# Layer norms of a six-block network on one core: the squares summed by token quarters, the root and its inverse on 128 columns, the inverse spread by a product, the gate columns summed last

## The chip, the cores and the metric

The kernel runs on one core of one Trainium2 chip. The metric is the device time of one launch in microseconds (us), the median of three runs. The matrix engine is called PE here (its weight loads PEld), the vector engine DVE, the scalar engine ACT, GpSimd POOL, and the queue of weight loads SP. Memory in front of PE's output is PSUM, in banks of 128 partitions by 512 float32 values.

## The reference, cut to what matters

A residual stream x of 512 tokens by 1024 channels goes through four mixer layers (MLA, sliding window, sparse, MLA), a norm, and then two blocks of a second network (hybrid attention and state space with a context of 256 tokens, FFN, short convolution, FFN). In front of each of the eight sublayers x is normed over its channels and modulated:

```python
def rmsnorm(x, g):
    xf = x.astype(jnp.float32)
    y = xf * lax.rsqrt(jnp.mean(xf * xf, axis=-1, keepdims=True) + RMS_EPS)
    return (y * g.astype(jnp.float32)).astype(x.dtype)
...
        shift, scale, gate = jnp.split(cond @ ada_w[i] + ada_b[i], 3, axis=-1)
        h = rmsnorm(x, norm_g[i]) * (1 + scale[:, None, :]) + shift[:, None, :]
...
        x = x + gate[:, None, :] * y
```

There are two more norms of x without modulation (the end of the first network and of the second), one of the context, and in each MLA layer two small ones (of q_a with 256 channels and of kv_a with 128). All values are float32.

## The kernel before, in words

x lies with channels on partitions: eight tiles of 128 channels by 512 tokens. A mean over channels is therefore a sum over partitions, and PE makes it: a product of a 128 by 128 matrix of ones with the squares puts each token's sum on all 128 partitions of a PSUM bank, 512 columns wide. The trace records each float32 product as two MATMUL passes, so a line with x2 is one product.

Each engine has its program written out by hand, in order, and semaphores connect them. What happens at the border between two sublayers, where the change lies:

- The last product of a sublayer (`out_projection`, or the FFN's down chunks) makes x tile by tile. DVE adds each tile to x (`add_result`, L2206), ACT squares it (L1599), and DVE adds up the squares of tiles 0 to 6 in `sq_sum`.
- `result_squares` on PE (L767 to L782) sums `sq_sum` with the ones (L770), then four columns of the modulation, then the squares of the last tile (L778) into the same bank. The modulation columns (`column_sums`, L751) are the next sublayer's shift, scale and gate: POOL has summed weight times condition over the channel tiles in `ada_sum`, and PE sums each of 24 blocks of 128 over its partitions. Columns 0 to 15 are shift and scale, 16 to 23 the gate, which is not needed before the end of the sublayer. All 24 go into one tile. Two products of the identity (`fill`, L764) follow, whose result nothing reads.
- ACT takes the root of the 512 columns (`root_of_squares`, L1609), DVE the reciprocal (`normed`, L2052, or `final_norm`, L2067) into the bank RB. Then DVE adds the biases to the 24 columns (`mod_columns`, L2042), makes the gains (L2044), and makes h in eight steps of 128 by 512 (L2061): x times gain times RB. ACT adds the shift to each (`shift`, L1531), and PE's next product waits for the first of them and takes the eight, one after the other.

`final_norm` of the first network is special: x is normed in place (L2072), ACT squares it again (L1519), PE sums each of the eight squares by itself (`sum_squares`, L746), then turns the context (L1415), which DVE copies, and sums its squares (L1419). Then DVE norms both (`normed(5)`, `normed(4)`), and ACT shifts both. In the MLA layers the two small norms take ones products at L925 and L709, reciprocals at L2229 and products of two tiles of the gate (`gate(0, i)`) between them and their use.

PE's product tiles go to two PSUM banks in turn (`next_tile`, `evacuated`, `tile_used`). POOL starts the next sublayer's modulation when DVE tells `mods_ready`; SP starts a weight load when PE tells `slot_begun`.

Of the kernel before, what the change touches and what calls it, by code (L numbers as in the profile page):

```python
# [19 lines left out]
P = 128  # L20
T = 512
D = 1024
KT = D // P
TT = T // P
CTX = 256
# [211 lines left out]
def build(nc, A, out, tables, const):  # L237

    ctx = ExitStack()
    with ctx:  # L240
# [92 lines left out]
        def view(first, *shape):  # L333
# [4 lines left out]
            if len(shape) == 3:  # L338
# [13 lines left out]
                 "ada_step", "ada_product", "mods_ready", "dve_step", "act_step", "sq_ready", "sq_done", "square_given", "sum_step", "sum_done", "rms_ready",  # L352
# [320 lines left out]
        def _(pe):  # L673
# [69 lines left out]
            def sum_squares(i, first=False, part=T):  # L743

                pe.wait_ge(S["sq_ready"], n.take("sq_ready"))
                pe.matmul(SB[0][:, 0:part], ones, sq[:, i % 2, 0:part], start=first, stop=True,  # L746
                          skip_group_check=True).then_inc(S["sq_done"], 1)
# [158 lines left out]
            def mla(first=False):  # L906
# [16 lines left out]
                for i in range(2):  # L923
                    pe.wait_ge(S["lora_sq"], n.take("lora_sq"))
                    m = pe.matmul(tile.at, ones, sq[:, i, :], start=(i == 0), stop=(i == 1))  # L925
                m.then_inc(S["tile_done"], 1)
                pe.wait_ge(S["lora_sq"], n.take("lora_sq"))
                product(lambda k: ones, lambda k: probs[:, 0, 0:T], 1)
                for i in range(2):
                    gate(0, i)  # L930
# [423 lines left out]
            def ffn(job):  # L1354
# [7 lines left out]
                                lambda k, i=i: sum0 + 3 * i + k) for i in range(2)]  # L1362
                first_parts(chunks[0], slot_begins=False, fresh=h0)
# [45 lines left out]
            def block2_tensor():  # L1409
                for k in range(KT):  # L1410
# [5 lines left out]
                    m.then_inc(S["tile_done"], 1)  # L1416
                for k in range(KT):
                    pe.wait_ge(S["sq_ready"], n.take("sq_ready"))
                    pe.matmul(SB[1][:, 0:CTX], ones, sq[:, k % 2, 0:CTX], start=(k == 0), stop=(k == KT - 1)  # L1419
                              ).then_inc(S["sq_done"], 1)  # L1420
# [6 lines left out]
                ffn(None)  # L1427

# [24 lines left out]
            first_columns()  # L1453
            pe.wait_ge(S["consts_in"], 16)
# [1391 lines left out]
```

## Time and profile before

| | |
|---|---|
| three runs | 3045.56, 3048.13 and 3053.22 us, median 3048.13 |
| the profiled execution | span 3043.8 us from first to last instruction |
| PE busy | 2856.9 us, 94% of the span |
| DVE, POOL, ACT busy | 45%, 35%, 22% |
| mean granted PE clock | 0.963 of full speed |

The profiled execution's own time is not listed beside its span; the span lies 4.3 us under the median of the runs. PE is busy nearly throughout, but a pass counts as busy whether or not its result is needed.

### The profile page before, as it was taken

How to read it: one execution, taken by the hardware profiler on the slowest of the kernel's cores; microseconds unless marked ns; L12 is line 12 of the kernel's file. 1: busy time of each engine (PE TensorE's matmuls, PEld its weight loads, DVE VectorE, ACT ScalarE, POOL GpSimd, SP SyncE). 2: the span in 40 equal slices, each digit the busy share in tenths (PEclk: the TensorE clock that was granted, in tenths of full speed). 3: DMA queues.
4: the chain of work that ended last, by engine and by line, in shares of the span. 5: the costliest groups of instructions: out<-in, count | busy, mean ns of one | idle time of the engine just before them, and what ended most of it. 6: DMA issues, size and time to landing. Idle time of an engine off the chain costs nothing.

```text
span 3043.8 us, 32692 instructions
## 1 busy us (share of the span) xinstructions
PE 2856.9 (94%) x11819; PEld 1879.8 (62%) x11819; DVE 1362.8 (45%) x2676; ACT 673.7 (22%) x1588; POOL 1071.6 (35%) x574
## 2 busy tenths in 40 slices
PE   6899999999999999998889978999999999999997
PEld 5455544475555544554557546578888544688886
DVE  7333366314555723334645155445365322433454
ACT  2232134122333411323223122211100100211101
POOL 4783484088370008805830000287000583000000
PEclk7999999989999999999898988999999999999999
DMA  7342342244231024322310100244222343222221
GB/s 235 119 128 79 105 127 72 82 136 118 77 97 35 15 83 128 114 70 77 93 46 14 55 14 14 90 153 144 87 89 87 125 158 104 69 83 91 89 87 66
DMA packets 244976, 278.21 MB, mean 91 GB/s; under 512 B 39251, under 2 KB 217696, under 8 KB 244736
## 3 DMA queue, kind: packets, MB, share of 16 engines
q1 hardware_dynamic: 215872, 175.56, 18.8%
q0 software_dynamic: 28224, 100.86, 10.3%
q8 instruction: 71, 1.16, 0.2%
q10 hardware_dynamic: 768, 0.30, 0.0%
q14 instruction: 41, 0.34, 0.0%
HBM read 274.59 MB, written 2.10 MB: 91 GB/s over the span
## 4 chain that ended last, share of the span: by engine, by line
PE 85%; DVE 6%; DMA 3%; issue 2%; ACT 2%; SPq 1%; POOL 1%; DVEq 0%; ACTq 0%; POOLq 0%
PE psum L709 26%; PE psum L1315 24%; PE psum L866 11%; PE psum L852 3%; PE psum L736 3%; PE psum L840 3%; PE psum L1142 2%; PE psum L1190 2%; PE psum L751 1%; PE psum L1160 1%; PE psum L990 1%; PE psum L991 1%; DMA ring<-in_ffn_w_gate 1%; PE psum L1282 1%; PE psum L1195 1%
## 5 line engine op out<-in xcount | busy, mean ns | idle before, releaser
L709 PE MATMUL psum<-h,ring 128*128 128x512 f32 (+1 forms) x1808 | 772.3, 585 | 23.3 <-ACT h L1531 16.6
L636 POOL DMA_DIRECT2D ada_ring<-in_ada_w x192 | 114.7, 597 | 1446.7 <-DVE gains L2044 1223.5
L709 PEld LDWEIGHTS psum<-h,ring 128*128 128x128 f32 x1808 | 343.3, 193 | 417.4 <-issue 407.0
L648 POOL TENSOR_SCALAR ada_ring<-ada_ring,cond 128x1024 f32<-128x1024 f32 x168 | 481.9, 2869 | 8.6 <-POOL ada_sum L652 1.9
L652 POOL TENSOR_TENSOR ada_sum<-ada_sum,ada_ring 128x1024 f32<-128x1024 f32 x168 | 395.8, 2356 | 14.9
L866 PE MATMUL psum<-og,ring 128*128 128x512 f32 x768 | 334.6, 595 | 2.3 <-DVE og L2574 2.0
L1315 PE MATMUL psum<-og,arena 128*128 128x256 f32 x1152 | 258.6, 379 | 1.7 <-ACT probs L1882 1.7
L866 PEld LDWEIGHTS psum<-og,ring 128*128 128x128 f32 x768 | 145.1, 191 | 183.0 <-issue 179.5
L1315 PEld LDWEIGHTS psum<-og,arena 128*128 128x128 f32 x1152 | 218.7, 190 | 32.1 <-issue 2.4
L1315 PE MATMUL psum<-h,ring 128*128 128x256 f32 x768 | 178.3, 383 | 0.9 <-ACT h L1531 0.9
L1555 ACT ACTIVATE psum<-psum,neg_max 128x256 f32<-128x256 f32 (+4 forms) x288 | 150.1, 521 | 111.8 <-DVE neg_max L2126 85.4
L1566 ACT ACTIVATE probsT<-psum 128x128 f32<-128x128 f32 (+3 forms) x232 | 104.2, 449 | 300.3 <-PE psum L840 299.5
L1315 PEld LDWEIGHTS psum<-h,ring 128*128 128x128 f32 x768 | 145.6, 191 | 26.9 <-ACT h L1531 4.9
L1599 ACT ACTIVATE sq<-x 128x512 f32<-128x512 f32 x63 | 39.7, 630 | 428.9 <-DVE x L2206 232.7
L1882 ACT ACTIVATE probs<-psum 128x256 f32<-128x256 f32 x132 | 50.5, 383 | 369.7 <-PE psum L1315 369.7
L2664 DVE SCALAR_TENSOR_TENSOR x<-psum,mods,x 128x256 f32<-128x256 f32 x168 | 81.2, 483 | 112.0 <-PE psum L1315 110.8
L840 PE MATMUL psum<-cst,arena 128*128 128x128 f32 x608 | 112.3, 286 | 20.1 <-ACT probsT L1566 10.8
L2206 DVE SCALAR_TENSOR_TENSOR x<-psum,mods,x 128x512 f32<-128x512 f32 x48 | 36.0, 751 | 205.1 <-PE psum L866 204.6
L2140 DVE CUSTOM_DVE_ANT_0 psum<-psum,cst 128x128 f32<-128x128 f32 (+1 forms) x192 | 94.6, 499 | 72.6 <-PE psum L991 33.9
L852 PEld LDWEIGHTS psum<-probsT,arena 128*128 128x128 f32 x704 | 91.5, 196 | 38.7 <-issue 15.5
L1505 ACT ACTIVATE arena<-psum 128x512 f32<-128x512 f32 (+4 forms) x100 | 55.4, 557 | 268.9 <-PE psum L709 234.6
L1315 PE MATMUL psum<-h,arena 128*128 128x256 f32 x480 | 113.4, 379 | 0.0
(332 smaller groups left out, 3885.7 us busy)
## 6 DMA issues: line engine op xcount, KB each, us to landing
ada_ring<-in_ada_w POOLq DMA_DIRECT2D x192, 512.0 KB, 4.2
ring<-in_ffn_w_gate SPq DMA_DIRECT2D x22, 1024.0 KB, 5.4
ring<-in_ffn_w_up SPq DMA_DIRECT2D x22, 1024.0 KB, 5.4
ring<-in_ffn_w_down SPq DMA_DIRECT2D x16, 1024.0 KB, 4.9
ring<-in_sc_w_in SPq DMA_DIRECT2D x12, 1024.0 KB, 5.2
ring<-in_mla_w_in SPq DMA_DIRECT2D x10, 1024.0 KB, 5.5
ring<-in_mla_w_out SPq DMA_DIRECT2D x8, 1024.0 KB, 5.0
ring<-in_swa_w_in SPq DMA_DIRECT2D x16, 512.0 KB, 5.3
```

The lines of the kernel that those rows point to most:

```text
L636: pool.dma_start(ada_ring[:, i % 2, :], w[k * P:(k + 1) * P, first(part)]).then_inc(arrived[i % 2], n.give(f"ada_in{i % 2}", 16))
L648: step = nc.gpsimd.tensor_scalar(piece, ada_ring[:, i % 2, :], c, None, ALU.mult)
L652: step = nc.gpsimd.tensor_tensor(total, total, piece, ALU.add)
L709: m = pe.matmul(tile.at[:, part], lhs(k), rhs(k), start=(k == 0), stop=(k == K - 1))
L736: m = pe.matmul(tile.at[:, i * width:(i + 1) * width], h[:, k, j * P:(j + 1) * P], w8(slot, first, width)(k), start=(k == 0), stop=(k == K ...
L840: m = pe.transpose(bank[:, i * P:(i + 1) * P], p[:, block_at:block_at + P], ident)
L852: m = pe.matmul(o[:, q * P:(q + 1) * P], v(u, key), pT[:, i * P:(i + 1) * P], start=begin, stop=last, skip_group_check=True)
L866: m = pe.matmul(out_tiles[c].at, w8(out_slots[0], P * (c % 2))(k), og[:, k * T:(k + 1) * T], start=(k == 0), stop=(k == KT - 1))
L1315: last = pe.matmul(out, weights[:, k, :], moving[:, k, :], start=begins and k == 0, stop=True, skip_group_check=True)
L1555: e = nc.scalar.activation(scored, scored, ACT.Exp, bias=neg_max[:, step % 4, g:g + 1], scale=scale, accum_out=row_sum[:, step % 4, g:g + 1])
L1566: c = nc.scalar.activation(probsT[:, i % 2, 0:w], PB[:, 0:w], ACT.Copy)
L2140: last = nc.vector.tensor_tensor_reduce(s[:, at:at + w], s[:, at:at + w], mask(u), -scale, floor, ALU.add, ALU.min, neg_max[:, b, g:g + 1])
```

## The change

- Sums. `token_sums` replaces each product with ones by four, one for each quarter of the tokens: 32 columns of ones as weights, 128 tokens (64 for the context) as the moving side, written to partitions 32q to 32q+31. The bank then holds 128 columns, and each quarter of the partitions its own tokens.
- Root and reciprocal. ACT's root and DVE's reciprocal (`give_inverse`, now in place in `rms`) take 128 columns (64 for the context) instead of 512 (256). The reciprocal comes out of `normed`.
- Spread. `spread` is new on PE: four products whose weights are one column of the identity repeated 128 times, which take partition 32q of the inverse to all partitions of columns 128q to 128q+127 of RB (for the small norms of SB[0] and SB[1]). It waits for `root_given`, and DVE's h steps wait for `inverse_spread`.
- Modulation columns. Eight instead of four lie between the two sums, eight behind them; then comes the spread; the eight gate columns go last, into a tile of their own, and take the place of the two `fill` products (which stay at the border whose columns are the context's). On DVE `border_columns` handles 16 columns before h, `border_gates` the gate's eight after h step 3 (after step 1 in front of an FFN), and tells `mods_ready` there.
- The FFN's first parts on PE wait until both product tiles are evacuated. At the first norm the reciprocal comes before the last first-layer slot is passed, and the spread after `first_columns`. In the MLA layers the two spreads lie between `gate(0, 0)` and `gate(0, 1)`.

The diff, cut to its core:

```diff
+            def token_sums(bank, squares, first, last, tokens=P):
+                for q in range(4):
+                    m = pe.matmul(bank[32 * q:32 * q + 32, 0:tokens], ones[:, 0:32], squares[:, q * tokens:(q + 1) * tokens],
+                                  start=first, stop=last, skip_group_check=True)
+                return m
+            def spread(bank, inverse, tokens=P):
+                for q in range(4):
+                    m = pe.matmul(bank[:, q * tokens:(q + 1) * tokens], ident[:, 32 * q:32 * q + 1].broadcast_to([P, P]),
+                                  inverse[:, 0:tokens], start=True, stop=True, skip_group_check=True)
+                return m
+            def spread_inverse(bank=RB, tokens=P):
+                pe.wait_ge(S["root_given"], n.take("root_given"))
+                spread(bank, rms, tokens).then_inc(S["inverse_spread"], n.give("inverse_spread"))
...
             def result_squares(job, frees_slot=False):
-                added = pe.matmul(SB[0], ones, sq_sum[:, :], start=True, stop=False, skip_group_check=True)
+                added = token_sums(SB[0], sq_sum, True, False)
...
-                    column_sums(tile, range(4), False)
+                    column_sums(tile, range(8), False)
...
-                pe.matmul(SB[0], ones, sq[:, 1, :], start=False, stop=True, skip_group_check=True
-                          ).then_inc(S["sum_done"], 1)
+                token_sums(SB[0], sq[:, 1, :], False, True).then_inc(S["sum_done"], 1)
                 if job is not None:
-                    column_sums(tile, range(4, 16 if job == CTX_JOB else 24), True)
-                    fill(2)
+                    column_sums(tile, range(8, 16), True)
+                    spread_inverse()
+                    if job == CTX_JOB:
+                        fill(2)
+                    else:
+                        column_sums(next_tile(), range(16, 24), True)
...
+                for bank in (0, 1):
+                    evacuated_last(bank)
                 first_parts(chunks[0], slot_begins=False, fresh=h0)
...
-                nc.scalar.activation(rms[:, :], SB[0], ACT.Sqrt, bias=C["eps"], scale=1.0 / D
+                nc.scalar.activation(rms[:, 0:P], SB[0][:, 0:P], ACT.Sqrt, bias=C["eps"], scale=1.0 / D
...
+            def give_inverse(root=rms, tokens=P):
                 dve.wait_ge(S["rms_ready"], n.take("rms_ready"))
-                settle(nc.vector.reciprocal(inv, root))
+                nc.vector.reciprocal(root[:, 0:tokens], root[:, 0:tokens]).then_inc(S["root_given"], n.give("root_given"))
+            def normed(job, source=None, part=slice(0, T), inv=RB, columns=None):
                 if columns is not None:
-                    mod_columns(*columns)
+                    border_columns(*columns)
                 if job == 0:
                     first_columns()
-                else:
-                    dve.wait_ge(S["mods_ready"], n.now("mods_ready"))
+                dve.wait_ge(S["inverse_spread"], n.take("inverse_spread"))
                 for k in range(KT):
...
+                    if columns is not None and k == (1 if job in (6, 8) else 3):
+                        border_gates(columns[0])
```

## Rows read from the trace of the kernel before

**Rows 1.** The page: span, busy time of each engine.

```profile
span 3043.8 us, 32692 instructions
...
PE 2856.9 (94%) x11819; PEld 1879.8 (62%) x11819; DVE 1362.8 (45%) x2676; ACT 673.7 (22%) x1588; POOL 1071.6 (35%) x574
```

**Rows 2.** The chain that ended last, 325 to 337 us (start, us, what).

```profile
329.20 4.48 PE psum L751 x40
...
333.78 0.20 DVE mods L2042
```

**Rows 3.** Timeline of that border (start, us, engine, line, operation, idle before).

```profile
328.10 1.11 PE L778 MATMUL psum<-sq,cst 128*128 128x512 f32 x2
329.24 0.69 ACT L1609 ACTIVATE rms<-psum,cst 128x512 f32<-128x512 f32 x1 [1.22 <-PE psum L778]
330.03 3.36 DVE L2052 RECIPROCAL psum<-rms 128x512 f32<-128x512 f32 x1 [2.73 <-ACT rms L1609]
334.20 5.36 DVE L2061 SCALAR_TENSOR_TENSOR h<-x,gains,psum 128x512 f32<-128x512 f32 x8
334.83 0.61 POOL L636 DMA_DIRECT2D ada_ring<-in_ada_w  x1 [78.26 <-DVE gains L2044]
335.85 7.10 PE L709 MATMUL psum<-h,ring 128*128 128x512 f32 x16 [0.46 <-ACT h L1531]
```

**Rows 4.** DVE's groups by form (busy us, mean ns of one).

```profile
L2310 DVE RECIPROCAL arena<-arena 128x192 f32<-128x192 f32 x1 | 1.4, 1354 | 0.0
L2436 DVE RECIPROCAL arena<-arena 128x96 f32<-128x96 f32 x1 | 0.8, 755 | 0.0
```

**Rows 5.** ACT's groups by form: the root of the context's norm.

```profile
L1917 ACT ACTIVATE arena<-psum,cst 128x256 f32<-128x256 f32 x1 | 0.5, 473 | 0.8 <-PE psum L1419 0.8
```

**Rows 6.** PE's groups by form; 128*64 is weights of 64 columns.

```profile
L852 PE MATMUL psum<-probsT,arena 128*128 128x128 f32 x704 | 100.9, 286 | 4.8 <-ACT probsT L1563 3.6 <-ACT probsT L1566 0.9
...
L1160 PE MATMUL psum<-probsT,arena 128*64 128x128 f32 x640 | 49.3, 284 | 3.0 <-ACT probsT L1566 3.0
```

**Rows 7.** Timeline of PE: four products on 64-column weights, then 128-column ones.

```profile
401.79 0.66 PE L1042 MATMUL psum<-probsT,arena 128*64 128x128 f32 x8
402.38 0.44 PE L840 MATMUL psum<-cst,arena 128*128 128x128 f32 x2
```

**Rows 8.** Timeline of an FFN border.

```profile
1947.91 0.38 SPq L490 DMA_DIRECT2D ring<-in_ffn_w_up  x1
1956.24 8.66 PE L1315 MATMUL psum<-h,ring 128*128 128x256 f32 x32 [0.46 <-ACT h L1531]
```

**Rows 9.** The page: weight loads (KB each, median us from issue to landing).

```profile
ring<-in_ffn_w_up SPq DMA_DIRECT2D x22, 1024.0 KB, 5.4
```

**Rows 10.** Timeline of the border between the two networks.

```profile
1393.67 5.35 DVE L2072 SCALAR_TENSOR_TENSOR x<-x,cols,psum 128x512 f32<-128x512 f32 x8
1395.25 7.78 PE L746 MATMUL psum<-sq,cst 128*128 128x512 f32 x16 [0.27 <-ACT sq L1519]
1403.07 0.69 ACT L1524 ACTIVATE rms<-psum,cst 128x512 f32<-128x512 f32 x1 [1.22 <-PE psum L746]
1421.54 13.11 PE L709 MATMUL psum<-h,ring 128*128 128x512 f32 x32 [10.35 <-ACT h L1531]
```

**Rows 11.** Timeline of the last norm.

```profile
3018.28 1.10 PE L770 MATMUL psum<-sq_sum,cst 128*128 128x512 f32 x2 [1.27 <-DVE sq_sum L2692]
...
3024.38 5.36 DVE L2072 SCALAR_TENSOR_TENSOR x<-x,cols,psum 128x512 f32<-128x512 f32 x8
```

**Rows 12.** Timeline of the start: PE waits for POOL.

```profile
95.38 3.68 PE L751 MATMUL psum<-cst,ada_sum 128*128 128x128 f32 x16 [2.70 <-POOL ada_sum L652]
```

**Rows 13.** Engines by window: busy us, granted clock (PEclk).

```profile
326.00:336.00 10.00, 9.54 (x59) 7.06 (x58) 6.26 (x7) 2.34 (x4) 0.61 (x1) 1.00 0.01 2
1404.00:1421.00 17.00, 6.34 (x28) 3.44 (x26) 15.84 (x25) 11.69 (x25) 15.03 (x8) 0.76 0.29 91
...
75.00:82.00 7.00, 6.34 (x8) 2.74 (x9) 1.11 (x2) 1.23 (x2) 6.54 (x4) 0.51 0.41 134
```

More of the change, by code:

```diff
@@ L924, in mla @@
                     pe.wait_ge(S["lora_sq"], n.take("lora_sq"))
-                    m = pe.matmul(tile.at, ones, sq[:, i, :], start=(i == 0), stop=(i == 1))
+                    m = token_sums(tile.at, sq[:, i, :], i == 0, i == 1)
                 m.then_inc(S["tile_done"], 1)
+                tile = next_tile()
                 pe.wait_ge(S["lora_sq"], n.take("lora_sq"))
-                product(lambda k: ones, lambda k: probs[:, 0, 0:T], 1)
+                token_sums(tile.at, probs[:, 0, 0:T], True, True).then_inc(S["tile_done"], 1)
+                gate(0, 0)
                 for i in range(2):
-                    gate(0, i)
+                    pe.wait_ge(S["lora_given"], n.take("lora_given"))
+                    spread(SB[i], lora_rms[:, i, :]).then_inc(S["lora_spread"], n.give("lora_spread"))
+                gate(0, 1)
                 evacuated(kpe)
@@ L1416, in block2_tensor @@
                     m.then_inc(S["tile_done"], 1)
+                spread_inverse()
                 for k in range(KT):
                     pe.wait_ge(S["sq_ready"], n.take("sq_ready"))
-                    pe.matmul(SB[1][:, 0:CTX], ones, sq[:, k % 2, 0:CTX], start=(k == 0), stop=(k == KT - 1)
-                              ).then_inc(S["sq_done"], 1)
+                    token_sums(SB[1], sq[:, k % 2, :], k == 0, k == KT - 1, CTX // 4).then_inc(S["sq_done"], 1)
+                pe.wait_ge(S["root_given"], n.take("root_given"))
+                spread(SB[1], ctx_rms, CTX // 4).then_inc(S["inverse_spread"], n.give("inverse_spread"))
                 hybrid()
@@ L2045, in mod_columns, with border_columns, border_gates @@
                                                ).then_inc(S["mods_ready"], n.give("mods_ready"))
-            def normed(job, source=None, part=slice(0, T), root=None, inv=None, columns=None):
-                width = part.stop - part.start
-                root, inv = (rms[:, :], RB) if root is None else (root, inv)
+            def border_columns(job, g):
+                tile = next_tile()
+                done(tile)
+                b = col("ada_b", 24 * job, 16) if job < 4 else col("ada_b_2", (0, 0, 24, 48, 72)[job - 4], 16)
+                nc.vector.tensor_tensor(mods[:, job, 0:16], tile.at[:, 0:16], b, ALU.add).then_inc(tile_used[tile.bank], 1)
+                evacuated(tile)
+                last = nc.vector.scalar_tensor_tensor(gains[:, job, :], mods[:, job, 8:16], 1.0, g, ALU.add, ALU.mult)
+                if job == CTX_JOB:
+                    last.then_inc(S["mods_ready"], n.give("mods_ready"))
+                    dve.wait_ge(S["mods_ready"], n.now("mods_ready"))
+                else:
+                    settle(last)
+            def border_gates(job):
+                if job == CTX_JOB:
+                    return
+                tile = next_tile()
+                done(tile)
+                b = col("ada_b", 24 * job + 16, 8) if job < 4 else col("ada_b_2", (0, 0, 24, 48, 72)[job - 4] + 16, 8)
+                nc.vector.tensor_tensor(mods[:, job, 16:24], tile.at[:, 16:24], b, ALU.add).then_inc(tile_used[tile.bank], 1)
+                evacuated(tile)
+                dve.sem_inc(S["mods_ready"], n.give("mods_ready"))
+            def give_inverse(root=rms, tokens=P):
                 dve.wait_ge(S["rms_ready"], n.take("rms_ready"))
-                settle(nc.vector.reciprocal(inv, root))
+                nc.vector.reciprocal(root[:, 0:tokens], root[:, 0:tokens]).then_inc(S["root_given"], n.give("root_given"))
+            def normed(job, source=None, part=slice(0, T), inv=RB, columns=None):
                 if columns is not None:
-                    mod_columns(*columns)
+                    border_columns(*columns)
                 if job == 0:
                     first_columns()
-                else:
-                    dve.wait_ge(S["mods_ready"], n.now("mods_ready"))
+                dve.wait_ge(S["inverse_spread"], n.take("inverse_spread"))
                 for k in range(KT):
@@ L2073, in final_norm @@
                                                    ).then_inc(S["x_normed"], n.give("x_normed"))
+                    if k == 3 and columns is not None:
+                        border_gates(columns[0])
             def take_raw():
@@ L2228, in mla @@
                     evacuated(next_tile())
-                    settle(nc.vector.reciprocal(SB[i], lora_rms[:, i, :]))
+                    nc.vector.reciprocal(lora_rms[:, i, 0:P], lora_rms[:, i, 0:P]).then_inc(S["lora_given"], n.give("lora_given"))
+                for i in range(2):
+                    dve.wait_ge(S["lora_spread"], n.take("lora_spread"))
                     for k in ((0, 1), (2,))[i]:
```

47 lines of the change are left out of this document (29 added, 18 removed).

## The prediction

> **What bounds the kernel now.** First the page [rows 1]: PE is busy 94% of the 3043.8 us, so at first sight only less PE work could help. The second view, the chain of waits over one border [rows 2], shows what such a share hides: the 40 passes of L751 that stand in the chain for 4.48 us are modulation columns, and DVE's `mods` waits for the last of them. PE is busy there, but x waits. The third view is the timeline of that border [rows 3], and the reader should measure one stretch in it: from the start of ACT's root (329.24) to the first h step (334.20) 4.96 us pass, and to PE's next product (335.85) 6.61. Two chains run side by side in it. One is root 0.69, reciprocal 3.36, which ends at 333.39. The other is the 20 columns behind the second sum, 0.224 us each, which end at about 333.7. Shortening the reciprocal alone would thus win nothing: both must shrink. Seven borders have this form, at about 330, 595, 1124, 1389, 1950, 2377 and 2607 us, and the end at 3020 has no columns. DVE, ACT and POOL bound nothing here. I sum changes of the span; the runs' median lies 4.3 us over it, and I carry that over.
>
> **Sums.** A 512-column product takes (7.10 - 0.17) / 8 = 0.87 us of PE's issue [rows 3], where 0.17 is the tail of the last pass: a 128-column pass lasts 286 ns [rows 6], and the next starts 4.48 / 40 = 0.112 us after it [rows 2]. Four products of 128 columns would take 4 x 0.224 = 0.89 if they ran in turn. Whether 32-column products at four partition quarters run side by side no row shows, but a near one does: two streams of 64-column weights. 640 passes of L1160 cover 49.3 us, 77 ns each, 704 full ones of L852 100.9 us, 143 ns each, at the same mean duration [rows 6]; and four such products are done in 0.66 us from first to last [rows 7], against 4 x 0.224 + 0.17 = 1.07 in turn. So halves overlap. For quarters the bounds are 0.44 us (all four together) and 1.07 (in turn); I take 0.44, as a quarter is the same form cut once more, so 0.22 of issue.
>
> Going in and out of the narrow form costs something: in rows 7 the next full product starts 0.59 us after the first narrow pass, where four slots of 0.11 make 0.44, so 0.15 for both ways. A border has two such groups. The Trainium skill's page "TensorEngine Tiling (Array Packing)", section Tiling Modes, says that changing the tiling mode drains the engine, which speaks against mixing narrow and full products as this border does; the trace agrees by the 0.15 us. Its page "TensorE: Matmul & The Clock Gate", Part 3, gives 2.38 times for three column tiles; scaled to four that would be an estimate of 0.89 / 3.2 = 0.28 us of issue instead of 0.22, and a sum 1 us smaller.
>
> At 330: the first group takes 0.22 + 0.15 instead of 0.87 (-0.50), four more columns +0.90, the last group 0.44 + 0.05 to go in instead of 1.11 with its wait (-0.62). Its squares are there at 328.10, and PE comes to it at 328.5. The root starts some 0.1 us earlier (0.2 at 2377).
>
> **Root, inverse, spread.** Call the root's start T. ACT: 0.69 us at 512 columns [rows 3] and 0.473 at 256 [rows 5] make 0.37 at 128. DVE's reciprocal: 755 ns at 96 and 1354 at 192 [rows 4] make 0.955 at 128 instead of 3.36. With three hand-overs of 0.1 (329.93 to 330.03 in rows 3) PE may start to spread at T + 1.6. PE meanwhile does eight columns, 8 x 0.224 = 1.79, from T - 0.1: it is free at T + 1.7. So the columns hide the root and reciprocal, with 0.1 to spare; without them PE would stand still. The spread is four full products, 0.90 of issue and 0.17 of tail: h can start at T + 2.8, while `border_columns` (two short DVE steps, 0.2 each [rows 2]) is done at T + 2.2. Before, it was T + 4.96. **Gain at 330 and 595: 4.96 - 2.8 + 0.1 = 2.3 us each.**
>
> **Behind the start of h.** PE's first product needed 335.85 - 334.20 = 1.65 us after h begins, which makes T + 4.45. The eight gate columns behind the spread end at T + 2.6 + 1.8 = T + 4.4, so they replace the fills at no cost, hidden by that first h step and its shift; each 0.1 they were late would show in full. `border_gates` after step 3 makes the later steps 0.25 us late; PE takes a step per 0.87 us and DVE makes one per 0.67, so four steps' lead hides it. POOL hears `mods_ready` at T + 5.7, the 334.8 of before; it had waited 78 us for it [rows 3].
>
> In front of an FFN `border_gates` comes after step 1. The gate tile is done at T + 4.55, steps 0 and 1 already at T + 4.1, so DVE stands 0.7 us with six h steps queued behind it, and PE's two new waits for the tiles end at T + 4.8. PE takes these steps as they come (half as many tokens per pass), so nothing hides it: **1950 and 2607 gain 2.3 - 0.7 = 1.6 each.** The FFN's second weights are issued at 1947.91 and used from 1956.24 on [rows 8]; now PE wants them 1.6 earlier, 6.7 us after the issue. A load takes 5.4 [rows 9], so it stays hidden; were it late, the lateness would be lost.
>
> **The other places.** 1124 has 16 columns before as after and keeps its fills, so there the reciprocal alone set h: 0.69 + 0.1 + 3.36 and two short steps, 4.6 after the root. The gain is 4.6 - 2.8 + 0.1 = **1.9**. 2377 is as 330 with 0.1 more: **2.4**. 3020: two groups from 3018.28 on end at 3018.28 + 0.44 + 0.22 = 3018.9; 0.37, 0.955, the spread's 1.07 and three hand-overs lead to x at 3021.65 instead of 3024.38 [rows 11]: **2.7**.
>
> 1389: x starts 2.2 us earlier. From x to the root then took 1403.07 - 1393.67 = 9.4 us, because the eight sums, a product each, ran one behind the other for 7.78 [rows 10]. With 0.44 per group DVE's pace sets it: the first sum starts 1.58 after x [rows 10], seven more steps of 0.67, the 0.25 of `border_gates`, a group and a hand-over put the root at 7.1, 2.3 earlier. Behind it DVE's reciprocal and spread (0.955 + 1.2 for 3.36) win 1.2 more; but that spread stands ahead of the context's sums on PE, and ACT takes the root of the context before its sixteen shifts, the last of which lets PE go on at 1421.54. So between 0 and 3.5 of this arrives; I take 1.9, near the 2.3 of the sums, which lie ahead of all that. **Together 4.1.**
>
> First norm (42): the spread comes behind the columns and costs 0.4 to 0.7, but PE waits 2.70 us for POOL at 95.38 [rows 12], which swallows it. MLA's small norms: three sums cost 2.6 us of PE before, now 0.75 and two spreads 1.8: **0**; the reciprocals were beside the gate products and stay there.
>
> **Sum:** 2 x 2.3 + 1.9 + 4.1 + 2 x 1.6 + 2.4 + 2.7 = 18.9 us. Span 3043.8 - 18.9 = 3024.9; median 3048.1 - 18.9 = **3029**.
>
> **Rivals.**
> *The narrow sums run in turn.* Then each of two groups per border costs 0.67 more: 2.3 becomes 1.0, 2.4 becomes 1.1, 1.9 becomes 0.6, 1.6 becomes 0.3, 3020 gives 1.4, and 1389 keeps 2.0 (its eight sums stay as slow). Sum 7.4, time 3041, within 0.3%. For it: no row with four quarters. Against it: rows 6 and 7. Chance 0.10.
>
> *PE's clock falls at the borders.* Now it is 1.00 from 326 to 336, where PE is busy 9.54 of 10 us; it is 0.76 from 1404 to 1421 with 6.34 of 17, and after PE's idle stretch in the 7 us from 75 on, when PE had waited for DVE, it is 0.51 [rows 13]: 1.2 instead of 2.4 GHz, and half of such a stretch, some 3 us, is lost. Were it to fall at each border, the columns and the spread on the path would double too, 2.7 more: 5.7 per border, eight times, 46 us. Less the 18.9 that is 3075, slower. The mechanism decides from (18.9 + 9.1) / 8 = 3.5 us per border on. Against it: PE has queued work across each border, as before. The Trainium skill's page "TensorE: Matmul & The Clock Gate", Part 1, says that the lower level is the default and activity lifts it. Chance 0.07: 0.04 slower, 0.03 with a smaller fall, no change.
>
> *Something else eats it* (weights late, a wait between `border_gates` and the product tiles): 0.05, of which 0.02 no change, 0.01 slower.
>
> **How the numbers follow.** This measurement tells 0.3%, 9.1 us, from no change. My forecast (0.78) is faster by 14 to 26 us, 3022 to 3034. Faster 0.78 + 0.02 = 0.80; same 0.10 + 0.03 + 0.02 = 0.15; slower 0.05. The range takes in the serial rival and the runs' scatter of 3 us: 3021 to 3041.
>
> **What would show it.** Reciprocals of 128x128 near 0.955 us; narrow groups of eight passes in about 0.44 us; h 2.8 us after each root; granted clock 1.00 at the borders; PE without idle time in front of the spread. Groups of 1.07 us, or clocks under 1, would make the prediction wrong.

## The result and the profile after

The changed kernel took 3026.81 us in the median (3021.97 to 3029.63, four runs), the kernel before 3046.85 beside it: a ratio of 0.9933, 95% interval 0.9914 to 0.9951. 3029 had been predicted, in a range of 3021 to 3041. The profiled execution lasted 3021.97 us, its span 3020.0, which is 23.8 less than the span of before.

The border near 330 is now the one near 325. The timeline below answers to [rows 3]; its columns are the same.

```profile
324.65 0.43 PE L746 MATMUL psum<-sq_sum,cst 128*32 128x128 f32 x8
325.01 2.05 PE L769 MATMUL psum<-cst,ada_sum 128*128 128x128 f32 x16
...
326.99 0.42 PE L746 MATMUL psum<-sq,cst 128*32 128x128 f32 x8
...
327.35 2.05 PE L769 MATMUL psum<-cst,ada_sum 128*128 128x128 f32 x16
327.49 0.37 ACT L1640 ACTIVATE rms<-psum,cst 128x128 f32<-128x128 f32 x1 [1.25 <-PE psum L746]
327.95 0.95 DVE L2106 RECIPROCAL rms<-rms 128x128 f32<-128x128 f32 x1 [2.44 <-ACT rms L1640]
...
329.24 1.06 PE L753 MATMUL psum<-rms,cst 128*128 128x128 f32 x8
...
330.13 1.95 PE L769 MATMUL psum<-cst,ada_sum 128*128 128x128 f32 x16
330.40 2.72 DVE L2117 SCALAR_TENSOR_TENSOR h<-x,gains,psum 128x512 f32<-128x512 f32 x4 [0.59 <-PE psum L753]
...
332.05 2.38 PE L709 MATMUL psum<-h,ring 128*128 128x512 f32 x5
```

From the root to h it is now 2.91 us, where [rows 3] had 4.96, and to PE's next product 4.56 instead of 6.61. The spread of L753 starts 1.75 us after the root, when the sixteenth column is through PE; the reciprocal had ended 0.34 earlier. The gate columns end where the next product begins. PE doesn't stand still at any point, as the view by windows says (PE's busy time first, the granted clock behind POOL's):

```profile
322.00:333.00 11.00, 11.00 (x82) 8.16 (x81) 4.64 (x8) 2.82 (x5) 0.00 (x0) 1.00 0.01 3
```

The border between the two networks looks different. This is its timeline, which answers to [rows 10] and goes on to PE's next product:

```profile
1380.02 0.37 ACT L1555 ACTIVATE rms<-psum,cst 128x128 f32<-128x128 f32 x1 [0.66 <-PE psum L746]
...
1385.02 0.94 DVE L2106 RECIPROCAL rms<-rms 128x128 f32<-128x128 f32 x1
...
1386.02 2.08 PE L753 MATMUL psum<-rms,cst 128*128 128x128 f32 x8 [1.38 <-DVE rms L2106]
...
1391.76 0.31 ACT L1948 ACTIVATE arena<-psum,cst 128x64 f32<-128x64 f32 x1 [0.44 <-PE psum L746]
1391.97 8.18 ACT L1562 ACTIVATE h<-h,mods 128x512 f32<-128x512 f32 x16
```

The spread takes 2.08 us instead of 1.06: between 1380 and 1390 the granted clock was 0.51, the lower of the two levels (1.2 GHz). ACT's sixteen shifts then follow one another without a stop.

To see where the time went I measure each border from the first sum group to PE's next product (at the end, to the last norm's first step), and the stretches between from there to the next first sum group. Of either kernel a second profile was taken (the first experiment), so each gain is there twice:

| border | predicted | first profiles | second profiles |
|---|---|---|---|
| 330, 595 | 2.3 each | 2.10, 2.09 | 2.10, 2.11 |
| 1124 | 1.9 | 1.74 | 1.75 |
| 1389 | 4.1 | 2.17 | 4.65 |
| 1950, 2607 | 1.6 each | 1.66, 1.66 | 1.65, 1.66 |
| 2377 | 2.4 | 2.08 | 2.08 |
| 3020 | 2.7 | 2.81 | 2.80 |
| sum | 18.9 | 16.3 | 18.8 |
| the rest of the span | 0 | 7.5 gained | 8.7 lost |
| span | 18.9 | 23.8 | 10.1 |

But for 1389, the borders came within 0.32 us of what was predicted; 1389 did in the second profiles, with 0.55 more, and gave about half in the first. What is left to explain is the rest, which has both signs.

### The profile page after: what moved, and what is told of

It is laid out like the page before. It is cut to its first block, busy times and chain, and to the rows that moved or that the text cites. A ratio compares the mean times of both kernels' runs of the same rounds, so it can differ in the third digit from the quotient of the medians.

```text
span 3020.0 us, 33392 instructions
## 1 busy us (share of the span) xinstructions
PE 2838.9 (94%) x12155; PEld 1882.9 (62%) x12155; DVE 1318.2 (44%) x2682; ACT 668.7 (22%) x1588; POOL 1069.3 (35%) x574
## 4 chain that ended last, share of the span: by engine, by line
PE 84%; DVE 5%; DMA 4%; issue 2%; ACT 2%; POOL 1%; SPq 1%; DVEq 0%; ACTq 0%; POOLq 0%
PE psum L709 26%; PE psum L1340 24%; PE psum L887 11%; PE psum L873 3%; PE psum L736 3%; PE psum L861 3%; PE psum L1167 2%; PE psum L1215 2%; PE psum L769 2%; PE psum L1185 1%; DMA ring<-in_ffn_w_up 1%; PE psum L1015 1%; PE psum L1016 1%; DMA ring<-in_ffn_w_gate 1%; PE psum L1307 1%
## 5 line engine op out<-in xcount | busy, mean ns | idle before, releaser
L648 POOL TENSOR_SCALAR ada_ring<-ada_ring,cond 128x1024 f32<-128x1024 f32 x168 | 480.4, 2859 | 8.5 <-POOL ada_sum L652 1.8
L652 POOL TENSOR_TENSOR ada_sum<-ada_sum,ada_ring 128x1024 f32<-128x1024 f32 x168 | 396.0, 2357 | 14.9
L1340 PEld LDWEIGHTS psum<-h,ring 128*128 128x128 f32 x768 | 146.2, 192 | 26.1 <-ACT h L1562 5.2
L1340 PE MATMUL psum<-og,ring 128*128 128x256 f32 x400 | 98.3, 389 | 17.1 <-DVE arena L2700 17.1
```

The lines of the kernel that those rows point to most:

```text
L648: step = nc.gpsimd.tensor_scalar(piece, ada_ring[:, i % 2, :], c, None, ALU.mult)
L652: step = nc.gpsimd.tensor_tensor(total, total, piece, ALU.add)
L1340: last = pe.matmul(out, weights[:, k, :], moving[:, k, :], start=begins and k == 0, stop=True, skip_group_check=True)
```

## The experiments

**Both kernels once more, unchanged.**

> The changed kernel once more, unchanged, for a second profile. Theory: the borders repeat to within 0.05 us (at the border near 330, 5.75 us from the start of the first sum group to the first step of h and 7.40 to PE's next product; near 1389, 27.7 us from the start of the first root to PE's next product or more, if the clock falls there again it is over 30), while the stretches between borders, whose code the change leaves as it was, move by several us in either direction, because the clock falls in other places. Then the 9 us of the span's gain that don't lie at the borders are scatter of the clock, and not the change. Rival: the stretches between the borders repeat to within 1 us as well; then the change itself makes them shorter and longer, and the cause has to be found.

> The kernel before once more, unchanged, for a second profile. Theory: its borders repeat (4.96 us from the root near 330 to h, 32.7 from the root near 1389 to PE's next product), and the stretches between borders move by several us against the first profile; a time within 0.3% of the first. Rival: the stretches repeat to within 1 us.

Measured: the changed kernel 3033.5 us beside 3046.96, ratio 0.9958 (0.9943 to 0.9974); the kernel before 0.9991 (0.9978 to 1.0004). The borders repeat to 0.01 us, but for 1389, where the same program needed 30.6 us from root to product in one profile and 28.2 in the other. The stretches moved:

| stretch between | before, twice | changed, twice | changed forms, all twelve |
|---|---|---|---|
| 330 and 595 | 255.8, 255.8 | 252.8, 254.2 | 252.5 to 255.9 |
| 595 and 1124 | 519.8, 516.6 | 513.7, 516.8 | 513.7 to 520.2 |
| 1124 and 1389 | 255.9, 255.2 | 253.9, 257.0 | 253.1 to 261.9 |
| 1389 and 1950 | 525.2, 525.6 | 523.0, 523.2 | 521.7 to 529.3 |
| 1950 and 2377 | 417.7, 418.8 | 422.7, 427.8 | 422.7 to 429.4 |
| 2377 and 2607 | 219.8, 219.8 | 219.9, 219.9 | 219.8 to 219.9 |
| 2607 and 3020 | 405.5, 406.9 | 407.6, 409.6 | 405.5 to 409.6 |

(The last column takes in all kernels of this study but the two before.) Most rows overlap, which fits scatter, as the theory said. The first FFN, behind 1950, does not: 3.9 us longer or more in every changed form. There the rival holds, and the theory's "all scatter" is wrong. The second FFN, behind 2607, in which POOL does nothing, overlaps.

**One half alone.** The narrow form without the order, and the order without the narrow form:

```diff
-                    column_sums(tile, range(8, 16), True)
+                    column_sums(tile, range(8, 16 if job == CTX_JOB else 24), True)
                     spread_inverse()
-                    if job == CTX_JOB:
-                        fill(2)
-                    else:
-                        column_sums(next_tile(), range(16, 24), True)
+                    fill(2)
```

> From the changed kernel: narrow sums, root and reciprocal on 128 columns and the spread stay, but all 24 modulation columns lie ahead of the spread again and the two fill products behind it. Theory (PE's queue of columns sets h once the reciprocal is short): near 330 the spread starts eight columns (1.8 us) later than in the changed kernel, h 7.5 us after the start of the first sum group instead of 5.75 (7.85 before), so only 0.3 us of the 2.1 at such a border is left; 1.7 near 1124 and 2.8 at the end stay, near 1389 less than 1. In all about 7 us, 3040 us. Rival (the reciprocal was the bound, the columns' order is a detail): h 5.8 to 6.2 us after the first sum group, and some 14 us of gain are kept, 3033 us or less.

From the kernel before:

```diff
-                    column_sums(tile, range(4, 16 if job == CTX_JOB else 24), True)
-                    fill(2)
+                    column_sums(tile, range(4, 16), True)
+                    if job == CTX_JOB:
+                        fill(2)
+                    else:
+                        column_sums(next_tile(), range(16, 24), True)
```

> From the kernel before: only the gate's eight columns go last, into their own tile, with the two-part handling on DVE; sums, root and reciprocal stay 512 columns wide, and there is no spread. Theory (the 512-column reciprocal then sets h): h 4.6 us after the root starts instead of 4.96, so 0.36 us per border at four borders, less in front of an FFN, nothing near 1124 and at the end: 2 us in all, within 0.3% of before, and PE idle for more than 1 us ahead of its next product. With the narrow form alone the two gains add up to 9 us and not to the 15 that the whole change wins at the borders. Rival (the columns alone were the bound): h 2.8 to 3.2 us after the root, 10 us or more gained.

Measured: ratios 0.9990 (0.9975 to 1.0005) and 0.9996 (0.9981 to 1.0010). Timeline of the narrow form alone, then of the order alone:

```profile
331.29 0.37 ACT L1635 ACTIVATE rms<-psum,cst 128x128 f32<-128x128 f32 x1 [1.25 <-PE psum L746]
331.76 0.95 DVE L2081 RECIPROCAL rms<-rms 128x128 f32<-128x128 f32 x1 [2.44 <-ACT rms L1635]
334.83 1.06 PE L753 MATMUL psum<-rms,cst 128*128 128x128 f32 x8
...
335.99 2.72 DVE L2092 SCALAR_TENSOR_TENSOR h<-x,gains,psum 128x512 f32<-128x512 f32 x4 [0.58 <-PE psum L753]
```

```profile
329.40 0.69 ACT L1614 ACTIVATE rms<-psum,cst 128x512 f32<-128x512 f32 x1 [1.22 <-PE psum L778]
330.19 3.36 DVE L2082 RECIPROCAL psum<-rms 128x512 f32<-128x512 f32 x1 [2.73 <-ACT rms L1614]
...
335.87 1.52 PE L709 MATMUL psum<-h,ring 128*128 128x512 f32 x3 [2.04 <-ACT h L1536]
```

In the first the inverse is ready at 332.71 and waits 2.1 us for PE's columns: h is 4.70 us after the root, 7.53 after the first sum group (7.5 expected). In the second PE stands idle for 2.04 us: h comes 7.71 after the first sum group, PE's product 9.36 (9.50 before; near 595 it is 9.13, the 0.36 us that was expected). Near 330 the halves win 0.31 and 0.14 us, together they win 2.10. Both rivals have fallen.

**Without the gate columns.**

```diff
-                        column_sums(next_tile(), range(16, 24), True)
```

> From the changed kernel: PE leaves out the eight gate columns behind the spread at the seven borders, and DVE writes the bias alone as the gate, so the gates lack the product of weights and condition. Theory (the gate columns fill time in which PE would wait for h): h starts 5.75 us and PE's next product 7.40 us after the first sum group near 330, as with them; in front of the FFNs, near 1927 and 2584, PE comes 0.4 us earlier and the first steps of h run without the 0.7 us stop; in all 1 us, no difference that the times can tell. Rival 1 (the columns delay PE): its next product comes up to 1.8 us earlier at each border, 12 us in all. Rival 2 (they keep the clock up): the granted clock falls below 1.00 behind the borders, and the stages get longer by up to 3 us each.

Measured: 5.75 and 7.40 us near 330, as with them; 7.41 instead of 7.84 in front of both FFNs; and the time has a ratio of 0.9957 (0.9941 to 0.9973), that of the changed kernel. Near 330 the clock is 1.00 at the border and in the 10 us behind it, so there rival 2 is wrong: the columns are free where four steps of h hide them. Behind both FFN borders the clock does fall. These are the 10 us from PE's first product of the first FFN on, with the gate columns (first profile of the changed kernel), then without:

```profile
1931.41:1941.41 10.00, 9.60 (x38) 6.75 (x39) 9.79 (x11) 4.37 (x8) 4.03 (x3) 1.00 0.36 105
```

```profile
1954.51:1964.51 10.00, 9.72 (x35) 7.72 (x36) 9.79 (x11) 4.80 (x8) 4.16 (x3) 0.83 0.35 107
```

Without the columns PE stood still for 1.77 us ahead of that product, and the granted clock behind it was 0.83 instead of 1.00, in front of the second FFN as well. That took back the 0.43: from the first sum group to PE's first product of `og` with `ring`, some 16 us into the FFN, it is 23.67 and 23.57 us without the columns and 23.52 with them. So in front of an FFN, too, the columns cost nothing that lasts.

**The border between the two networks.** Three edits. The order (DVE's reciprocal of x ahead of the eight copies, PE's spread behind the second transposed tile, the context's reciprocal within h):

```diff
+                give_inverse()
                 for k in range(KT):
                     copy_tile(ctxT[:, k, :], CTX)
-                give_inverse()
-                normed(5)
-                give_inverse(ctx_rms, CTX // 4)
+                normed(5, between=lambda: give_inverse(ctx_rms, CTX // 4))
```

> From the changed kernel, at the border between the two networks alone: DVE takes the reciprocal of x ahead of the eight copies of the context instead of behind them, PE its spread behind the second transposed tile, and DVE the context's reciprocal behind the sixth step of h instead of behind the eighth. Theory (what is lost there is that DVE waits for two spreads, 1.2 and 2.1 us, which the kernel before didn't have): from the second root near 1390 to PE's next product some 15.8 us instead of 18.3 (second profile of the changed kernel) or 20.6 (first), 2.5 us won; all else as it is. Rival (the place is bound by the shifts of ACT or by the context's sums): within 0.5 us of 18.3.

Products that keep PE busy, without and with that order; the two kinds, and one of the places:

```diff
+            def warm_narrow(bank):
+                for q in range(4):
+                    pe.matmul(bank[32 * q:32 * q + 32, 0:P], ones[:, 0:32], ident, start=True, stop=True, skip_group_check=True)
+            def warm(bank, products=1):
+                for _ in range(products):
+                    pe.matmul(bank.rearrange("p (a b) -> p a b", b=P), ident, ident.unsqueeze(1).broadcast_to([P, TT, P]),
+                              start=True, stop=True, skip_group_check=True)
...
                 sum_squares(k, first=(k == 0))
+                if k < KT - 1:
+                    warm_narrow(SB[1])
```

> From the changed kernel, at the border between the two networks alone: products that nothing reads fill PE's gaps (a narrow group behind each sum of x and of the context's squares, 64 columns behind each pair of transposes, one 512-column product ahead of the first spread, two ahead of the second, five behind it). Theory (the clock falls there because PE stands idle between the short groups, and the cold second spread is on the path of DVE): granted clock 1.00 up to PE's next product, the second spread 1.0 us instead of 1.97, the product's first steps at full clock, 17.2 us from the second root to PE's next product instead of 18.3, and no profile with 20.6. Rival (the fill products delay the sums, or the clock falls anyway): 18.3 us or more.

> Both edits of the border between the two networks together (the order of the reciprocals, and products that fill PE's gaps). Theory: some 15.5 us from the second root to PE's next product with the clock at 1.00; 3 to 5 us less than the changed kernel in all, 0.1 to 0.15%, which the times can hardly tell from it; against the kernel before a ratio near 0.993. Rival: the fill products take back what the order wins, 18 us.

And, on top of the order, the context's sums between the transposes:

```diff
                     m.then_inc(S["tile_done"], 1)
+                    if k > 2:
+                        context_sums(k - 3)
```

> From the kernel with the new order at the border between the two networks: in addition the sums of the context's squares lie between the transposes on PE (each three tiles behind) instead of behind all of them. The theory of the spreads has fallen; the new one is: ACT takes the context's root and then its sixteen shifts without a stop, 8.84 us from that root to PE's next product in each of the five profiles of the changed form, so what counts is how late the context's sums are, and these lie behind the spread on PE. Expected: the context's root 6 us after the second root instead of 8.56, the sixteen shifts then bound by DVE's steps of h (5.4 + 5.36 + 0.55 + 3.22 us after the root), and PE's next product some 15.5 us after the second root instead of 17.40 (18.29 and 20.58 in the changed kernel). Rival (DVE or the spreads set it): 17.4 as before this edit.

Measured, from the second root (of x) to the context's root, to PE's next product, and the granted clock in that stretch:

| kernel | context's root | PE's product | clock |
|---|---|---|---|
| changed, first profile | 11.74 | 20.58 | 0.58 |
| changed, second profile | 9.45 | 18.29 | 0.81 |
| order | 8.56 | 17.40 | 0.73 |
| fill products | 9.53 | 18.38 | 1.00 |
| order and fill products | 8.70 | 17.54 | 1.00 |
| order and early sums | 9.03 | 18.28 | 0.69 |

Two theories fell here. The order won 0.89 us and not 2.5 (17.40; 15.8 was the theory, 17.8 to 18.8 the rival). DVE's waits for the spreads don't set the end: with fill products the second spread took 1.10 us instead of 1.97, and PE's product came no earlier (18.38). The distance between the last two columns is 8.84 or 8.85 in the first five rows: ACT takes the context's root, then sixteen shifts (8.2 us) without a stop, so only a later or earlier root of the context counts in these rows. Where the clock is low the root is late (11.74): the transposes of the context and the first spread, which lie ahead of the context's sums on PE, then take longer. The kernel with the early sums did not show their gain: in its profile the clock fell (the first spread took 2.07 us). The last experiment shows it at a clock of 1.00.

**The first FFN.** While it runs, POOL makes the next modulation: it loads weights (512 KB), multiplies them (L648) and adds them up (L652). What makes the FFN longer stands in the timeline of DVE, POOL and PE behind the load of the FFN's own gate weights. First the kernel before (second profile), then the changed one (first profile):

```profile
1978.85 0.96 DVE L2587 TENSOR_TENSOR arena<-ring 128x512 f32<-128x512 f32 x1 [5.89 <-DMA ring<-in_ffn_w_gate]
...
1981.05 0.69 DVE L2594 TENSOR_TENSOR arena<-ring,arena 128x512 f32<-128x512 f32 x1
1981.08 2.87 POOL L652 TENSOR_TENSOR ada_sum<-ada_sum,ada_ring 128x1024 f32<-128x1024 f32 x1
...
1982.13 1.99 PE L1315 MATMUL psum<-og,ring 128*128 128x256 f32 x8 [2.41 <-DVE arena L2638]
```

```profile
1957.33 0.69 DVE L2649 TENSOR_TENSOR arena<-ring 128x512 f32<-128x512 f32 x1 [7.13 <-DMA ring<-in_ffn_w_gate]
...
1958.83 2.59 POOL L652 TENSOR_TENSOR ada_sum<-ada_sum,ada_ring 128x1024 f32<-128x1024 f32 x1
1959.27 2.71 DVE L2656 TENSOR_TENSOR arena<-ring,arena 128x512 f32<-128x512 f32 x1
...
1962.37 2.07 PE L1340 MATMUL psum<-og,ring 128*128 128x256 f32 x4 [5.40 <-DVE arena L2700]
```

DVE makes four sums of the weights, 0.69 us each, when they land. Before, the fourth began 0.03 us ahead of POOL's addition, and POOL's was the one that got longer (2.87 instead of 2.35). In the changed kernel DVE's first sum began 6.61 us after the load's issue (1950.72) instead of 5.37 (5.61 in the first profile of before), POOL's addition came ahead of the fourth sum by 0.44, and that sum took 2.71. PE waited 5.40 us instead of 2.41, and its clock over the next 7 us (1962 to 1969) was 0.67 instead of 1.00. One DVE sum of 2.7 to 2.8 us, and a wait of PE of 4.1 to 8.0, stand in all twelve profiles of changed forms, and in neither of the two of before.

How much of the lost time lies there can be read from the weight loads, which SP issues as PE takes up the weights. From the issue of the gate weights to the next one it is 11.22 and 11.23 us in the two profiles of before, 16.32 and 15.95 in those of the changed kernel, and 15.15 to 19.03 in all twelve. From there to the thirteenth load (the gate weights are the first) it is 145.1 and 146.2 before, 143.9 to 146.5 in eight of the twelve and 150.2 to 151.0 in the other four (the second profile of the changed kernel is one); from that load to the next border it is 242.3 in all fourteen. So the 5 us of the first profile lie at this one place, and of the 9 us of the second 4.7; the others come later in the FFN, in four profiles of twelve.

The kernel without the gate columns shows the meeting without a late load: its weights were there early (first sum 5.34 us after the issue), but POOL's addition came 7.08 us after it instead of 7.59, met the fourth sum (7.27, 2.71 us long), and PE waited 4.12. What counts is thus the distance between the two.

Two tries to move POOL out of the way:

```diff
                 evacuated(tile)
-                dve.sem_inc(S["mods_ready"], n.give("mods_ready"))
+                if job != 6:
+                    dve.sem_inc(S["mods_ready"], n.give("mods_ready"))
...
                         border_gates(columns[0])
+                    if job == 6 and k == 3:
+                        dve.sem_inc(S["mods_ready"], n.give("mods_ready"))
```

> From the changed kernel: at the border of the first FFN alone, DVE tells POOL that the modulation is ready behind the fourth step of h instead of the second, so POOL starts some 1.4 us later against PE. Theory (the first FFN got 5 to 10 us longer because POOL's fourth addition now starts 0.4 us ahead of DVE's last weight sum, which then takes 2.7 us instead of 0.69, PE waits 5.4 instead of 2.4 us, and the clock falls behind that wait): POOL's addition now comes behind DVE's four sums, the last of which takes 0.7 us, PE's wait is 2.4 us again, and the stretch from PE's first product of this FFN to the next border is 418 to 421 us instead of 423 to 428. Rival 1 (later encounters of POOL and DVE in the same stretch decide): that wait goes, but the stretch stays at 422 or more. Rival 2 (the weight load, which took 6.6 instead of 5.6 us, decides): PE's wait stays above 4 us.

Measured: 0.9948 (0.9930 to 0.9966), but POOL began 0.57 us behind PE's first product, as it had (0.56): the increment, no part of an instruction, went out before the step ahead of it had ended. As an experiment it is void; as one more profile of the changed kernel it showed DVE's first sum 7.88 us after the load's issue and PE waiting 7.99. So it was tried again with the increment on a copy:

```diff
-                        dve.sem_inc(S["mods_ready"], n.give("mods_ready"))
+                        nc.vector.tensor_copy(mods[:, job, 16:24], mods[:, job, 16:24]).then_inc(S["mods_ready"], n.give("mods_ready"))
```

> From the changed kernel, at the border of the first FFN alone, as in the run before, but now the tell to POOL hangs on an instruction of DVE (a copy of the eight gate columns onto themselves behind the fourth step of h) and not on a bare increment, which went out 1.3 us ahead of the steps in front of it and left POOL where it was (0.57 us behind PE's first product, 0.56 in the changed kernel). Theory (the encounter of POOL's fourth addition with DVE's four weight sums decides): POOL starts some 2.2 us behind PE's first product, its addition 9.3 to 9.9 us after the gate weights are issued instead of 8.2, behind the start of DVE's last sum (7.3 to 8.7 there); all four sums take 0.7, PE's gap is 2.4 to 3.7 us instead of 4.1 to 8.0, and the stretch to the next border takes 418 to 422 us instead of 423 to 428. Rival 1 (later encounters decide): the gap goes, the stretch stays at 422 or more. Rival 2 (the weight load, 5.4 to 7.9 us long, decides): the gap stays above 4 us.

```profile
1953.74 0.37 SPq L490 DMA_DIRECT2D ring<-in_ffn_w_gate  x1
...
1961.42 0.69 DVE L2652 TENSOR_TENSOR arena<-ring 128x512 f32<-128x512 f32 x1 [8.20 <-DMA ring<-in_ffn_w_gate]
...
1962.55 2.37 POOL L652 TENSOR_TENSOR ada_sum<-ada_sum,ada_ring 128x1024 f32<-128x1024 f32 x1
1962.63 2.83 DVE L2657 TENSOR_TENSOR arena<-arena,ring 128x512 f32<-128x512 f32 x1
```

Now POOL's addition came 8.81 us after the issue (8.11 in the changed kernel's first profile), but the weights came later too, after 7.68. It met the third sum, PE waited 6.59, the stretch took 423.0 us, and the time had a ratio of 0.9961 (0.9947 to 0.9975). The wait stayed above 4 us, the sign of rival 2, but the load is only half of it: of the 4.2 us that the wait is longer than before, 2.3 are the later weights and some 2 the sum that met POOL. The try moved both: over the fourteen profiles the load tends to be the longer, the shorter the time from POOL's own load to it (from issue to landing 5.3 us where POOL's was issued 3.1 us earlier; 5.3 to 6.3 at 2.6; 6.2 to 7.9 at 2.0; 7.7 and 7.4 at 1.4 and 1.2). That the one makes the other isn't shown; no run moved POOL's load alone.

**All edits together.**

> The changed kernel with all edits that the runs point to: at the border between the two networks the reciprocals ahead of the copies and within h, the context's sums between the transposes, and products that keep PE busy; in front of the first FFN the late tell to POOL. Theory: the clock stays at 1.00 there, the context's root comes 6 to 7 us after the second root and PE's next product 15.5 to 16.5 instead of 18.3 to 20.6; the first FFN as in the run with the late tell. Together 6 to 9 us less than the changed kernel, a ratio to the kernel before near 0.993 where the changed kernel has 0.9933 and 0.9958 in its two comparisons. Rival (the place scatters more than these edits win): no difference from the changed kernel.

Measured: 3027.2 us beside 3042.05, ratio 0.9943 (0.9929 to 0.9957). At the border of the networks the theory was right: clock 1.00, the context's root 7.19 us after the second root (6 to 7 expected), PE's product 16.08, where the order and the fill products without the early sums had 17.54. The first FFN was no better (PE waits 6.21 us; 429.4 for the stretch). In time it can't be told from the changed kernel, so I can't say that it beats it.

## Why the prediction was right, and where it was not

**Two chains side by side.** Right, and shown: each half alone wins 0.1 to 0.3 us near 330, both win 2.10.

**The sums.** A group of eight passes took 0.43 us (0.44 predicted), so the rival of sums in turn is out. In the last norm two groups stand one behind the other, 0.22 us apart:

```profile
2996.89 0.43 PE L746 MATMUL psum<-sq_sum,cst 128*32 128x128 f32 x8 [1.27 <-DVE sq_sum L2754]
2997.11 0.43 PE L746 MATMUL psum<-sq,cst 128*32 128x128 f32 x8
```

The Trainium skill's page "TensorE: Matmul & The Clock Gate", Part 3, gives 2.38 times for three column tiles, from which the prediction had an estimate of 0.28 for four; the trace decides for 0.22. From a group's start to the next column it is 0.36, so 0.14 for the change of form, where 0.15 was taken from [rows 7]. (The rival's gains add up to 7.7, not 7.4, and its time to 3040; nothing hangs on it.)

**Root, inverse, spread.** 0.37 and 0.95 as predicted. h came at 2.91 us instead of 2.8 and the root 0.06 earlier instead of 0.1; these two make 2.1 out of 2.3, and 1.75 out of 1.9 near 1124. The extra 0.1 near 2377 was not there.

**Behind h.** PE's product 4.56 after the root (4.45 predicted), the gate columns free, 1.65 in front of each FFN (1.6), 2.8 at the end (2.7). Of the 1.65 some 0.27 are lost again in the FFN's first products, whose steps of h come late behind `border_gates`: from PE's first product to the one with `og` and `ring` it is 15.68 us instead of 15.41. The gain that lasts is thus 1.39.

**1389.** The 4.1 was 4.65 in one profile and 2.17 in the other. The sums won what was said: from x to the second root 7.0 to 7.1 us instead of 9.4. Of the 3.5 us won behind x the prediction let "between 0 and 3.5" arrive and took 1.9; x itself came 2.0 us earlier, so 2.7 and 0.2 arrived. It named ACT's shifts as what lets PE go on, and that was the right place. Its sum had no term for a low clock there, which [rows 13] show before the change already and which can take the rest: the five profiles with this form of the border needed 20.58 and 20.83 us from the second root to PE's product at a clock of 0.58 and 0.50, and 18.29, 18.63 and 18.29 at 0.81, 0.69 and 0.80. PE stood still between the short groups in all of them; why the clock fell further in some, I can't explain.

**The step that failed** is that nothing behind a border changes: the FFN's weights "stay hidden". Those of the border's own products did. The gate weights some 20 us later did not: the first FFN gave back 5 us in one profile and 9 in the other. The prediction had weights that come late among "something else", at 0.05, but no term for DVE's sums of them. That POOL's addition and DVE's sum get in each other's way is shown by the fourteen profiles, and that 4 to 8 us are lost there by SP's next load, a part of them to the later weights. What brings them together is their distance: with a later load in eleven of the twelve, with an earlier POOL in the kernel without the gate columns. Why the load is longer in the changed forms, even with POOL in its old place (the narrow form alone, 5.88 us), stays open. Before, 0.03 us decided it. No run took POOL away from there, so that the 5 us would then come back isn't shown.

**The sum.** 18.8 us at the borders of the second profiles against 18.9; less 5 to 9 in the first FFN, and scatter of the other stretches, gives 10 to 24 in single profiles, 20.0 (3046.85 to 3026.81) and 13.5 (3046.96 to 3033.5) in medians. That the first median falls on the prediction is in part luck: of the ten comparisons of the changed kernel and of the forms close to it (ratios 0.9933 to 0.9961) it has the largest gain, and the second, 13.5, lies below the 14 to 26 that were forecast.

## What to carry to other kernels

Where two chains run side by side, price the change as a whole: here neither half wins anything that the time can tell. Follow each engine that starts earlier or later through the next stage, down to the first moment in which two engines get in each other's way; a margin of 0.03 us there is no margin. Take a second profile of both kernels before explaining a stretch that the change leaves alone.

## What the runs showed of the hardware

- Four products with 32 columns of weights on four partition quarters run fully side by side: 0.43 us for eight passes of 128 columns, 0.22 from group to group.
- An addition of DVE (128 by 512) that began while POOL was adding (128 by 1024) took 2.71 to 2.84 us instead of 0.69 at the place shown; begun 0.03 us ahead of POOL's, it kept its 0.69, and POOL's took 2.87 instead of 2.35. The Trainium skill's page "SBUF — State Buffer", section "SBUF: two separate sides", says that whichever of the two starts first, a DVE operation with two inputs from SBUF or a GpSimd one, holds a pair of ports for its whole instruction and the other stands still. The traces agree for these additions: from 1900 us on 80 sums of the fourteen profiles began in one of POOL's additions, and each ended 0.54 to 0.56 us behind it; 42 began ahead of one, and each took 0.68 or 0.69. They don't agree for POOL's products with one tensor (L648): of 315 sums that began in one 243 took no more than 0.70 us, the others up to 1.65, and those ended 1.2 us or more ahead of the product.
- A load of 1 MB on SP's queue took 5.3 to 7.9 us in the same place of the program, while POOL's own loads ran beside it.
- A bare increment in DVE's queue reached POOL 1.3 us before the vector instructions ahead of it had ended: POOL's load went out 0.57 us behind PE's first product, and 2.03 with the increment on a copy.
- With PE kept busy by products that nobody reads, the clock stayed at 1.00 through the border between the networks, in three profiles; in the others it was 0.50 to 0.81 there (mean of the stretch). In front of the FFNs the gate columns did the same: without them PE stood still for 1.77 us, and the clock of the next 10 us was 0.83 instead of 1.00.
